# Page values of a decoder step in four column groups of TensorE, a third buffer for value pages, and no stop of TensorE between retention heads

## The reference

```python
def gather_pages(cache_l, page_table):
    g = cache_l[page_table]
    return g.reshape(page_table.shape[0], -1, cache_l.shape[2], cache_l.shape[3])

def sb_attend(q, qpos, k, v, kpos, bias):
    z = (jnp.einsum('bqhd,bkhd->bhqk', q, k).astype(jnp.float32) * (HD_SB ** -0.5)
         + bias.astype(jnp.float32)[None, :, None, None])
    mask = kpos[None, :] < qpos[:, None]
    log_1m = jnp.where(mask, jax.nn.log_sigmoid(-z), 0.0)
    after = lax.cumsum(log_1m, axis=3, reverse=True) - log_1m
    a = jnp.where(mask, jnp.exp(jax.nn.log_sigmoid(z) + after), 0.0)
    return jnp.einsum('bhqk,bkhd->bqhd', a.astype(v.dtype), v)
```

## Time and profile before

| | us |
|---|---|
| median of 3 runs | 3448.25 (3447.4 to 3449.44) |
| the profiled execution, its own time | 3444.74 |
| its span in the profile | 3442.8 |
| of it the four heads, from head 0's first matmul to the end of head 3 | 356.03 |
| page pairs loaded, keys and values | 64 |

### The profile page before, as it was taken

One profiled execution on the slowest core, in us unless ns is written; L12 is line 12 of the kernel. 1 busy time (PEld: TensorE's weight loads), 2 busy tenths in 40 slices (PEclk: granted clock), 3 DMA queues, 4 the chain that ended last, 5 costly groups with the idle time before them and its releaser, 6 DMA issues.

```text
span 3442.8 us, 48372 instructions
## 1 busy us (share of the span) xinstructions
PE 3227.1 (94%) x19272; PEld 3008.2 (87%) x19272; DVE 1874.7 (54%) x2690; ACT 729.6 (21%) x933; POOL 1002.0 (29%) x452
## 2 busy tenths in 40 slices
PE   8999999969979999999999899999889999999996
PEld 5867777859958999999999899789769999999996
DVE  5344555563762655655565645446645645565556
ACT  2556312121021211111111211232222111111111
POOL 1211212104303433333333322123114333333331
PEclk9999999979999999999999999999999999999998
DMA  6110143343420111111111133524301111111111
GB/s 229 51 47 33 58 139 127 111 135 125 141 86 31 48 50 43 49 43 49 43 48 51 53 119 102 167 69 166 128 13 48 49 44 47 47 43 44 50 44 68
DMA packets 146842, 261.17 MB, mean 76 GB/s; under 512 B 34698, under 2 KB 89738, under 8 KB 144274
## 3 DMA queue, kind: packets, MB, share of 16 engines
q1 hardware_dynamic: 109058, 223.47, 19.6%
q10 hardware_dynamic: 37648, 35.71, 3.2%
HBM read 231.95 MB, written 27.18 MB: 75 GB/s over the span
## 4 chain that ended last, share of the span: by engine, by line
PE 78%; DVE 13%; issue 5%; ACT 2%; DMA 2%; DVEq 0%; SPq 0%; ACTq 0%
PE ps L530 64%; PE ps L882 2%; DVE cb L1434 2%; DVE Hl L1434 2%; PE ps L799 2%; DVE X L1430 2%; PE ps L629 1%; DVE tls L1438 1%; PE ps L970 1%; PE ps L618 1%; PE ps L674 1%; PE ps L687 1%; DVE accn L1430 1%; PE ps L588 1%; PE ps L664 1%
## 5 line engine op out<-in xcount | busy, mean ns | idle before, releaser
L506 POOL TENSOR_TENSOR Wh<-wraw,con 128x1024 fp32r<-128x1024 f32 x224 | 436.6, 1949 | 2374.8 <-PE ps L530 2308.1
L530 PE MATMUL ps<-Hh,Wh 128*128 128x344 f32 x4320 | 952.3, 329 | 30.8 <-DVE Hl L1430 8.5
L530 PE MATMUL ps<-Hh,Wl 128*128 128x344 f32 x4320 | 917.0, 321 | 5.9 <-issue 5.9
L530 PE MATMUL ps<-Hl,Wh 128*128 128x344 f32 x4320 | 920.6, 321 | 0.0
L530 PEld LDWEIGHTS ps<-Hh,Wh 128*128 128x128 f32 x4320 | 730.7, 189 | 70.4 <-issue 41.5
L530 PEld LDWEIGHTS ps<-Hl,Wh 128*128 128x128 f32 x4320 | 734.7, 190 | 0.0
L530 PEld LDWEIGHTS ps<-Hh,Wl 128*128 128x128 f32 x4320 | 724.8, 189 | 6.4 <-issue 6.4
L509 POOL TENSOR_TENSOR Wl<-wraw,Wh 128x1024 fp32r<-128x1024 f32 x224 | 565.2, 2523 | 17.6
L1430 DVE TENSOR_TENSOR X<-ps,X 128x1032 f32<-128x1032 f32 x200 | 244.2, 1229 | 332.0 <-PE ps L530 332.0
L1434 DVE SCALAR_TENSOR_TENSOR cb<-ub,fp,cb 128x1024 f32<-128x1024 f32 x176 | 338.1, 1921 | 90.6 <-ACT cb L1023 90.6
L1430 DVE TENSOR_TENSOR ub<-ps,rs 128x1032 f32<-128x1032 f32 x88 | 108.5, 1233 | 373.7 <-PE ps L530 373.6
(11 more groups left out here) (214 smaller groups left out, 2793.3 us busy)
## 6 DMA issues: line engine op xcount, KB each, us to landing
wraw<-in_wts SPq DMA_DIRECT2D x224, 512.0 KB, 3.5
mw<-in_memw SPq DMA_DIRECT2D x32, 512.0 KB, 3.8
pg<-in_ck SPq DMA_DIRECT2D x64, 256.0 KB, 2.8
pg<-in_cv SPq DMA_DIRECT2D x64, 256.0 KB, 2.7
X<-in_x SPq DMA_DIRECT2D x8, 1032.0 KB, 8.2
early<-in_cmk SPq DMA_DIRECT2D x16, 512.0 KB, 7.6
kv<-in_cmv SPq DMA_DIRECT2D x16, 512.0 KB, 3.4
late<-in_cmv SPq DMA_DIRECT2D x16, 512.0 KB, 4.1
```

The source lines that it names most:

```text
L506: pool.tensor_tensor(Wh[:, j, :], wraw[:, j, :], one.broadcast_to((P, 1024)), ALU.mult).then_inc(w_hi, 1)
L530: ins = mm(o, w[:, wcol[0], wcol[1]:wcol[1] + P], r, start=first and a == 0, stop=last and a == 2)
```

## The change

Five edits belong together. (1) Each of the four heads' page values goes to partitions 32h and 32h + 1 of bank 7, so to a column group of its own, in the same 128 columns. (2) ScalarE copies the four pairs of rows into `oc`, a tile cleared once at the start, and one matmul with picked columns of the identity turns all four. (3) Value pages use three buffers in turn: the two of `pg`, and `qb`, which is read for the last time by the page scores; pair 10 waits for the end of the scores alone. (4) PE drains and counts up at the end of a head and goes on; it waits for `r_rt` (the square root has read banks 3 to 5) before L734 and for VectorE's end before the transposes L739; it reads `sel` itself, so `selp` is gone. PE's heads are written out four times in place of a loop. (5) VectorE copies `hb` after the rotation.

```diff
+        def page_slot(m):
+            return m % 2 if m < 8 else (m - 8) % 3
+        def page(m):
+            return rt["pg"][:, page_slot(m), :, :] if page_slot(m) < 2 else rt["qb"][:, :, :]
+        def page_landed(i, m):
+            slot = page_slot(m)
+            before = sum(page_slot(n) == slot for n in range(m + 1))
+            return ss(f"ld_pg{slot}"), (224, 224, 64)[slot] * i + 32 * before
...
-                sp.wait_ge(pg_free, 16 * i + (m + 1))
+                sp.wait_ge(pg_free, 16 * i + (m + 1 if m < 10 else m))
...
-                pe.wait_ge(ss("r_cst"), 2 * i + 2)
+                if i:
+                    pe.wait_ge(ss("r_rt"), i)
                 for b in range(2):
-                    ins = mm(ps[:, 4 + b, :], rt["selp"][:, b, :], mx["qtok"][:, :], start=True, stop=True)
+                    ins = mm(ps[:, 4 + b, :], sel[:, 2 * i + b, :], mx["qtok"][:, :], start=True, stop=True)
                 ins.then_inc(ss("r_qb"), 1)
+                if i:
+                    pe.wait_ge(end_dve, i + E_SB)
...
-                    pe.wait_ge(ss(f"ld_pg{m % 2}"), 256 * i + 32 * (4 + m // 2 + 1))
+                    pe.wait_ge(*page_landed(i, 8 + m))
                     for n in (2 * m, 2 * m + 1):
                         b, g = n // PG, n % PG
                         for h in range(H):
-                            ins = mm(ps[0:2, 7, h * P:(h + 1) * P], zm[:, g, b, h, :],
-                                     rt["pg"][:, m % 2, n % 2, h * P:(h + 1) * P],
-                                     start=(n == 0 and h == 0), stop=(n == 15 and h == H - 1),
-                                     skip_group_check=True)
+                            ins = mm(ps[32 * h:32 * h + 2, 7, 0:P], zm[:, g, b, h, :],
+                                     page(8 + m)[:, n % 2, h * P:(h + 1) * P], start=n == 0, stop=n == 15)
...
-                pe.wait_ge(ss("y_oc"), i + 1)
-                for h in range(H):
-                    ins = mm(ps[:, 6, 2 * h:2 * h + 2], rt["junk"][0:2, h * P:(h + 1) * P],
-                             con[0:2, C_ID:C_ID + 2], start=True, stop=True)
-                ins.then_inc(ss("y_ot"), 1)
-                end_stage(pe, end_pe, i + (E_SB + 1))
+                pe.wait_ge(ss("y_oc"), H * (i + 1))
+                mm(ps[:, 6, 0:2 * H], rt["oc"][:, :], ident.rearrange("p (h r) -> p h r", h=H)[:, :, 0:2],
+                   start=True, stop=True).then_inc(ss("y_ot"), 1)
+                pe.drain().then_inc(end_pe, 1)
+                if not more:
+                    ended(pe, i + (E_SB + 1))
...
-            with pe.Fori(0, H - 1) as i:
-                head(i, True)
-            head(H - 1, False)
+            for i in range(H):
+                head(i, i < H - 1)
...
-                fn(rt["junk"][0:2, :], ps[0:2, 7, :], ACT.Copy, ss("y_oc"))
+                for h in range(H):
+                    fn(rt["oc"][32 * h:32 * h + 2, :], ps[32 * h:32 * h + 2, 7, 0:P], ACT.Copy, ss("y_oc"))
...
+            dve.memset(rt["oc"][:, :], 0.0).then_inc(ss("r_st0"), 1)
             def head(i):
                 hb, z = rt["hb"], rt["zz"]
-                fixed()
-                copy(hb[:, :], con[:, bass.ds(HB * i + C_HEAD, HB)], ss("r_cst"))
-                fixed()
-                copy(rt["selp"][:, :, :], sel[:, bass.ds(2 * i, 2), :], ss("r_cst"))
...
+                fixed()
+                copy(hb[:, :], con[:, bass.ds(HB * i + C_HEAD, HB)], ss("r_cst"))
                 dve.wait_ge(ss("r_qk"), 2 * i + 2)
```

More of the change, by code:

```diff
@@ L157, in build @@
                         ("kt_pad", [P, NS]), ("st", [P, TT + 1, P]), ("s0", [P, NS, P]),
-                        ("hb", [P, HB]), ("kvs", [NS, 2, P]), ("kms", [NS, NS, P]), ("selp", [NS, 2, P]),
+                        ("hb", [P, HB]), ("kvs", [NS, 2, P]), ("kms", [NS, NS, P]), ("oc", [P, P]),
                         ("pg", [P, 2, 2, H * P]), ("qb", [P, 2, H * P]), ("zz", [P, 8, 64]),
@@ L349, in pages @@
                                           max_val=NPAGES - 1) for p in range(2)]
-                sp.wait_ge(pg_free, 16 * i + (m + 1))
+                sp.wait_ge(pg_free, 16 * i + (m + 1 if m < 10 else m))
                 for p in range(2):
-                    load(rt["pg"][:, m % 2, p:p + 1, :], (cache_k, cache_v)[m // 8][bass.ds(at_pages[p], 1)]
-                         .rearrange("a p n -> p a n"), ss(f"ld_pg{m % 2}"))
+                    load(page(m)[:, p:p + 1, :], (cache_k, cache_v)[m // 8][bass.ds(at_pages[p], 1)]
+                         .rearrange("a p n -> p a n"), ss(f"ld_pg{page_slot(m)}"))
             def load_x(c):
@@ L1619, in head @@
                     tt_(x[:, :], rt["t1"][:, :], rt["t2"][:, :], ALU.add, ss("r_qk"))
+                fixed()
+                copy(hb[:, :], con[:, bass.ds(HB * i + C_HEAD, HB)], ss("r_cst"))
                 dve.wait_ge(ss("r_qk"), 2 * i + 2)
-                dve.wait_ge(ss("r_cst"), 2 * i + 1)
+                dve.wait_ge(ss("r_cst"), i + 1)
                 tt_(rt["qd"][:, :, :], rt["rq"][:, 0:T].rearrange("p (c n) -> p c n", c=TT),
@@ L1626, in page_scores @@
                 def page_scores(m):
-                    dve.wait_ge(ss(f"ld_pg{m % 2}"), 256 * i + 32 * (m // 2 + 1))
+                    dve.wait_ge(*page_landed(i, m))
                     for n in (2 * m, 2 * m + 1):
```

## The result

The changed kernel takes 3399.74 us (median of four; three of them lie between 3397.45 and 3399.86), the kernel before 3448.85 on the same chip: a ratio of 0.9855, 95% interval 0.9839 to 0.9871. The prediction said faster, by 34 us to 3414; it became some 49 us. 0.9855 of 3448.25 is 3398, a little under the range's lower end of 3399, and near the price of the rival "full overlap" (3401, chance 0.08). One of the four executions took 4530.64 us at a mean granted clock of 0.648; it is left out of the ratio, and the median without it is 3399.62. The profiled execution took 3397.45 us. Its lines are shifted: L734 is now L749, L739 L756, L747 L764, L768 L785, L799 L816, L588 L602, L819 L833, L530 L544; VectorE's L1430, L1434, L1699 are L1445, L1449, L1713, ScalarE's L1023 is L1037.

A forecast was written before the change was run, and what follows sets the result against it. PE bounds where it finishes last, as in page stages; VectorE and DMAs pace the last head. Stage terms summed to 321.7 us for the heads, 34.4 less than 356.03; from the median 3448.25 that gives 3414, range 3399 to 3436.

The forecast's parts named there:

- full overlap: Page values: rival that all four heads' passes run at once, page stages of 19.4 us, 3401 us; chance 0.08.
- likeliest case: Page values: half overlap, a block of 0.98 us in place of 1.74, by itself 3405 to 3424 us; chance 0.64.
- The two passes of one head share a group and must follow each other: Page values: only one head's second pass overlaps the next head's first; 0.76 us less a block, 6.0 a page stage.
- PE's heads as straight code: PE's loop over heads written out: taken as 0, a gain or loss under 1 us a head not foreseeable.
- End of a head to the key transposes: Heads 1 and 2: no stop, rg and VectorE's copy done in time, full clock; 0.6 + 14.25 = 14.9 us.
- Key transposes to the first page value: Heads 1 and 2: PE waits for VectorE's masked scores as in head 0; 44.8 us in place of 42.07.
- give-back: Heads 1 and 2, at L768: PE early, VectorE late, so part of the gain is lost; 44.77 us in place of 42.07.
- The third buffer: Value pages: gain taken as 0 in heads 0 to 2; it pays in the last head's end.
- cover gone: Value pages in heads 0 to 2: if lost, it would cost up to 1 us a stage.
- The last head's end: Last head's page stage and end: 19.3 us in place of 25.68, three pairs waiting ready, normalisation late next.
- Four copies of oc: ScalarE's copies behind the last chunk: between 0.59 and 4 x 0.59 us, the lower end taken.
- "slower" rival: Page values: each change of column group costs a pause; at 0.109 us each, 3458 us; chance 0.05.

The follow-up runs named there:

- e6: Kernel after with a block's matmuls ordered by head, then by page; 3400.98 us (one run).
- e12: Kernel before with only PE's four heads written out as straight code in place of the loop; 3442.95 us, ratio 0.9978.
- e10: Kernel before run again unchanged for a second profile; 3448.28 us (one run), heads 357.3 us.
- e1: Kernel after with page values of all heads back in one column group, one copy and four closing matmuls; 3428.27 us, ratio 0.9932.
- e5: Kernel after with two column groups of two heads each in place of four groups; 3406.9 us (one run).
- e8: Kernel after with the second column sum after the second block, not the fourth, and ScalarE's table load ahead of its wait for C; 3392.9 us, ratio 0.9833.
- e3: Kernel after with two buffers for value pages in place of three; 3407.07 us, ratio 0.9869.
- e9: Kernel after with only ScalarE's table load drawn ahead of its wait, column sums left in place; 3396.98 us, ratio 0.9843.

## Why the prediction was wrong

Its sign and its chain were right, and its likeliest case was not. Two steps failed; three terms were mis-sized. That the time came so near the range is partly luck, since the misses in the heads point both ways (the last paragraph has them). So is the nearness to the full-overlap rival's 3401: it had 308.7 us for the heads, which took 313.6, and the difference was made up by time gained outside of the heads, which it put at nothing.

**The failed step: "The two passes of one head share a group and must follow each other".** That they follow each other is right; that this holds up the next head's first pass is not. The block shrank by 3.45 - 2.17 = 1.28 us in place of 0.76, four groups at once, and the page stages by some 10 us in place of 6.0. In the sum: 3 x 23.4 = 70.2 forecast, 57.8 measured. The evidence of the earlier trace rows, two loads beside a running pass, spoke for this and was read for less than it showed; the order in the program was taken for the order of starts. The Trainium skill, "TensorE: Matmul & The Clock Gate", section "The mechanism", has matmuls start in strict order, and weight loads overlap running matmuls only where the row group differs. The traces disagree with both: in e6 passes of four groups start within 0.05 us although the four passes of one group stand next to each other in the order, and eight loads start with them while all of them use all 128 rows. The Trainium skill, "TensorEngine Tiling (Array Packing)", section "Theoretical Speedup", gives up to 4 times for so few columns: the trace agrees, 16 x 0.109 = 1.74 us became 0.46, 3.8 times.

**The other failed step: PE's heads as straight code, "I take 0".** By the medians e12 puts 6.6 us on it (4 to 11), and not in the heads, where the term was looked for (357.3 us, as in e10), but behind them. With 42.4 in the heads that makes the 49 that were timed. The profiles show less behind the heads, 2 to 3.5 us in e12 and 4 to 6 in the kernel after, and how straight code gains there is not shown.

**End of a head to the key transposes: 14.9 forecast, 19.5 and 20.2 measured.** That PE passes the end in 0.6 us and L749 runs at the full clock is right (0.4; 1.95 us). That rg and VectorE's closing copy are done by then holds for page stages of 29 us (e1: no wait), and for those of 22.5 us in e5 nearly (a wait of 0.4). With stages of 19 us they are not. The full-overlap rival saw this and gave it 1 us; it is 3.55, since C is not only 2 us late but doubled by POOL's split, and 1.28 us of table load stand behind it. At the ends of heads 0 and 1 the stretch took 9.9 us more than forecast: 7.0 of waiting and 3.6 of longer work at the lower clock, less 0.7 at the closing matmul. At the third end the wait costs little, since the last head's keys then wait 8.9 us for VectorE.

**Key transposes to the first page value: 44.8 forecast, 41.74 measured, twice.** The wait of L768 for VectorE in heads 1 and 2 did not come, because PE itself came late, at L756. Where page stages are short and PE hardly waits for rg the give-back is there: 44.5 and 45.95 us in e8, 45.9 and 46.5 in e5, which with its page stages of 22.5 us is nearest to the forecast. In e1, with stages of 29.4 us, PE does not wait for rg either, and there is none (42.4 and 42.2): VectorE is in time there. The mechanism was right; in the kernel after its condition was not met.

**The third buffer: 0 in heads 0 to 2, up to 1 us a stage with "cover gone".** Asked for every 19.4 / 8 = 2.4 us a pair is late with two buffers: in e3 that is some 2 us a stage. The last head's end was forecast at 19.3 with it and came to 17.7. The timeline of that end:

```profile
707.34 2.00 PE L602 MATMUL ps<-t,con 128*128 128x344 f32 x6
710.54 6.60 DVE L1713 RECIPROCAL rst<-rst 128x1032 f32<-128x1032 f32 x1 [6.87 <-ACT rst L1037]
710.76 3.41 SPq L347 DMA_DIRECT2D pg<-in_cv  x4
716.58 1.03 PE L816 MATMUL ps<-pg,zz 128*2 128x128 f32 x16 [1.16 <-DMA pg<-in_cv]
717.18 1.29 DVE L1449 SCALAR_TENSOR_TENSOR t<-t,hb,rst 128x1032 f32<-128x1032 f32 x1
718.62 1.23 DVE L1445 TENSOR_TENSOR C<-t,rg 128x1032 f32 x1
718.88 0.59 PE L833 MATMUL ps<-con,oc 128*128 128x8 f32 x2 [1.26 <-ACT oc L1037]
```

Counted from the first page value (702.33), the column sums came at 5.0 us where 6.6 were forecast, and the last pair was used at 14.3 where it was to land by 13.5: the blocks, short as they are, now wait for what SP issues (two pairs here in 3.41 us). Pages and normalisation end together, within a microsecond (717.6 and what follows it to 719.5; C to 719.85), so neither alone sets that end any more.

The rest is smaller. Four copies of oc took 1.15 us in place of 0.59 and lie beside the last chunk (483.69 to 484.84, before L833 at 485.00). The last head begins by its VectorE, 55.7 us against 53.2 forecast; what the 2.5 more are is not shown. The wait for rg need not be it: the same stretch takes 55.2 us in e1, without that wait, and 55.1 in e10, the kernel before. The "slower" rival fell: 192 changes of group cost nothing that shows. Against the forecast's 321.7 the heads took 313.6: 12.4 less in the page stages, 9.9 more at two ends of heads, 6.1 less behind them, 0.9 more in the last head, 0.4 less in head 0.

## What to carry to other kernels

Matmuls of few columns belong in different column groups, and their order in the program matters little: a block here cost the passes of its fullest group. When such a stage gets a third shorter, look at what ran beside it and follow its chain to the end (here the normalisation, a product that takes twice as long beside GpSimd's split, and a table load that a semaphore holds back): start that earlier in the same edit, as e8 does. And compare the stretches that an edit does not touch: a loop written out can change the time of loops elsewhere by as much as a real part of the change.

## What the runs showed of the hardware that was not expected

- Passes of different column groups overtake one another: four starts within 0.04 us with a head's two passes adjacent in the order, and within 0.05 us with four adjacent (e6). Two-column loads of all 128 rows ran beside them, eight in 0.11 us.
- ScalarE's table load is not drawn ahead of a wait: it stood 3.73 us for VectorE's C and then took 1.28. A function of the same table ahead of the wait took it out of the way (e9: 1.3 us less at each end).
- Waits without a visible cause, about 1 us each (the longest shown 1.5), moved between loops that run 0.5 and 2 ms after the code that was edited (e12). Their sum stayed nearly the same, 9.0 and 8.3 us.
